# A one-layer hybrid encoder on one core: dense weight remainders formed by VectorE alone, and the spatial gating bias added by VectorE from a broadcast tile

## The reference, cut to what matters

```python
xn = rmsnorm(x, norm_mix_g);  z = xn @ w_in            # q/k, v, o, gates, u, gv, mq, branch gates
qk = silu(causal_conv(qk_raw, conv_buf, w, b))          # mLSTM branch: matrix memory, 4 heads
...
u = gelu(u_raw);  gv = layernorm(gelu(gv_raw), gmlp_norm_g, gmlp_norm_b)
w_s = where(tri, gmlp_w_s[:, :cl, :cl], 0.0)            # cl = 128 for the prompt, 64 for the sample
sp = einsum('gts,bcsgd->bctgd', w_s, gvb) + gmlp_b_s[:, :cl].T[None, None, :, :, None]
br_gmlp = (u * sp) @ w_br_gmlp
...
x = x + (gates0 * br_mlstm + gates1 * br_gmlp + gates2 * br_mem) @ w_out
x = x + hier_moe(rmsnorm(x, norm_moe_g), ...)           # 32 experts of 1024 x 256, top 2 of a group of 8
```

## Time and profile before

| | |
|---|---|
| median of 3 runs | 993.53 us |
| the profiled execution | 991.24 us |
| its span (first to last instruction) | 989.5 us |
| mean granted clock of PE | 0.97 of full speed |
| PE busy | 898.8 us (91%) |
| DVE busy | 594.8 us (60%) |
| ACT busy | 473.1 us (48%) |
| POOL busy | 250.9 us (25%) |

### The profile page before, as it was taken

The page is one execution under the profiler, slowest core; times in us unless marked ns, Lnnn a source line. Parts: engine busy times, 40 slices in busy tenths (PEclk is TensorE's granted clock), DMA queues, the critical chain, the costliest instruction groups (busy, mean ns, idle before and its releaser), DMA issues.

```text
span 989.5 us, 13338 instructions
## 1 busy us (share of the span) xinstructions
PE 898.8 (91%) x5322; PEld 796.4 (80%) x5322; DVE 594.8 (60%) x794; ACT 473.1 (48%) x571; POOL 250.9 (25%) x161
## 2 busy tenths in 40 slices
PE   1889999888999989888999999869999999999993
PEld 0588998878989889888999999838877887787881
DVE  2734257884133254378354444584888889889874
ACT  4344345442433133334323333357777677767752
POOL 3145543333442444243443444100000000000000
PEclk9999999998999999989999999969999999999996
DMA  8225642333347856943423348204999999999951
GB/s 244 85 91 166 213 154 81 97 97 116 123 148 97 108 157 88 138 139 119 148 88 126 128 128 276 108 0 174 350 353 348 352 347 343 350 348 355 348 201 56
DMA packets 102502, 182.68 MB, mean 185 GB/s; under 512 B 8345, under 2 KB 74593, under 8 KB 102434
## 3 DMA queue, kind: packets, MB, share of 16 engines
q1 hardware_dynamic: 95488, 171.55, 54.2%
q0 software_dynamic: 2640, 7.66, 3.6%
q10 hardware_dynamic: 4306, 2.54, 1.3%
HBM read 175.90 MB, written 5.82 MB: 184 GB/s over the span
## 4 chain that ended last, share of the span: by engine, by line
PE 55%; DMA 10%; DVE 5%; ACT 4%; POOL 2%; issue 2%; DVEq 0%; SPq 0%; ACTq 0%
PE pj L526 25%; PE pj L776 14%; PE pj L798 8%; DMA arena<-in_w_in 8%; POOL unit_r L1586 2%; DMA arena<-in_w_exp_down 2%; ACT unit_r L882 2%; PE ms L812 1%; PE ms L700 1%; PE ms L699 1%; ACT w_r L889 1%; DMA arena<-in_w_exp_up 1%; PE ms L526 1%; PE ms L741 1%; DVE w_r L1183 1%
## 5 line engine op out<-in xcount | busy, mean ns | idle before, releaser
L1586 POOL TENSOR_TENSOR unit_r<-arena,unit_r 128x1024 fp32r<-128x1024 f32 x64 | 210.4, 3289 | 326.9 <-ACT unit_r L882 326.9
L526 PE MATMUL pj<-xn_r,unit_r 128*128 128x320 f32 x1536 | 237.3, 313 | 9.6 <-POOL unit_r L1586 9.0
L1183 DVE TENSOR_TENSOR w_r<-arena,w_r 128x2048 fp32r<-128x2048 f32 x96 | 218.9, 2289 | 44.5 <-ACT w_r L889 44.2
L526 PEld LDWEIGHTS pj<-xn_r,unit_r 128*128 128x128 f32 x1536 | 228.4, 190 | 14.1 <-issue 12.7
L1174 DVE TENSOR_TENSOR unit_r<-arena,unit_r 128x1024 fp32r<-128x1024 f32 x64 | 85.0, 1329 | 233.5 <-ACT unit_r L882 233.5
L889 ACT ACTIVATE w_r<-arena 128x2048 fp32r<-128x2048 f32 x96 | 183.5, 1917 | 46.1 <-DMA arena<-in_w_exp_up 30.7
L776 PE MATMUL pj<-w_r,xg 128*128 128x512 f32 x768 | 190.8, 398 | 0.0
L776 PEld LDWEIGHTS pj<-w_r,xg 128*128 128x128 f32 x768 | 141.9, 189 | 30.5
L882 ACT ACTIVATE unit_r<-arena 128x2048 fp32r<-128x2048 f32 x64 | 121.9, 1905 | 62.2 <-PE pj L526 28.9
L798 PE MATMUL pj<-w_r,hidT 128*128 128x512 f32 x384 | 93.1, 391 | 3.0 <-DVE w_r L1183 1.5
L798 PEld LDWEIGHTS pj<-w_r,hidT 128*128 128x128 f32 x384 | 71.6, 188 | 20.1 <-DVE w_r L1183 3.6
(11 more groups left out here) (303 smaller groups left out, 844.9 us busy)
## 6 DMA issues: line engine op xcount, KB each, us to landing
arena<-in_w_in SPq DMA_DIRECT2D x40, 1024.0 KB, 5.3
arena<-in_w_exp_gate SPq DMA_DIRECT2D x64, 512.0 KB, 4.5
arena<-in_w_exp_up SPq DMA_DIRECT2D x64, 512.0 KB, 6.0
arena<-in_w_exp_down SPq DMA_DIRECT2D x64, 512.0 KB, 5.2
arena<-in_w_mem_k SPq DMA_DIRECT2D x4, 1024.0 KB, 11.3
arena<-in_w_mem_v SPq DMA_DIRECT2D x4, 1024.0 KB, 6.3
arena<-in_w_br_mem SPq DMA_DIRECT2D x4, 1024.0 KB, 7.7
arena<-in_w_br_mlstm SPq DMA_DIRECT2D x4, 1024.0 KB, 5.0
```

The lines of the kernel that those rows point to most:

```text
L526: last = mm(bank_of(s)[0:out_rows, 0:out_cols], l, r, start=k == 0, stop=k == len(pairs) - 1)
L1183: v.tensor_tensor(w_r[u % NS][:, 1, :], raw_w[u % NS], w_r[u % NS][:, 0, :], ALU.subtract).then_inc(m_lo, 1)
L1586: g.tensor_tensor(unit_r[n % RING][:, 1, UW // 2:], ringw[:, n % RING, UW // 2:], unit_r[n % RING][:, 0, UW // 2:], ALU.subtract).then_inc ...
```

## The change

Two edits. First, DVE forms the whole rest of a dense unit (2048 columns), and POOL none; the two counters `u_lo` become one. Second, the bias of the spatial gating leaves PE: `bsb`, loaded on ACT's queue, holds gmlp_b_s in all 128 rows (256 KB in place of 2 KB). In an sp step DVE adds it to the bank's 256 prompt columns and 64 sample columns into `spb` (in the memory of `h_tm`, free once the heads are transposed), which frees the bank, waits for that, and multiplies `uT` by `spb`. ACT then waits for the product's own semaphore `s_spm`. The third tile's matmul runs over 128 rows, for which DVE zeroes rows 64 to 127 of `gv_tm`'s third tile ahead of the statistics.

```diff
@@ -354,7 +354,8 @@
         wr = sb("wr", [128, KC, G + E])
         wrb = sb("wrb", [G + E, 1])
         wif = sb("wif", [128, KC, 2 * H])
-        bs = sb("bs", [1, H * 128])
+        bsb = sb("bsb", [128, H, 128])
+        spb = at(XS, T)
         ws2 = sb("ws2", [128, 2 * H, 128])
         ws, wsT = ws2[:, 0:H, :], ws2[:, H:2 * H, :]
         nf_g = ws2[:, :, :].rearrange("p a b -> p (a b)")
@@ -411,12 +412,13 @@
         s_c1s = sem("C1_sample_ready")
         s_hn = sem("h_scaled")
         s_mix, s_wsT = sem("gate_used"), sem("wsT_masked")
+        s_bs, s_spm = sem("spatial_bias_loaded"), sem("u_gated")
         s_gng, s_gnd, s_gvout = sem("gn_loaded"), sem("gv_normed"), sem("gv_out")
 
         s_nfg, s_gm = sem("nf_g_loaded"), sem("moe_g_loaded")
         s_lgx, s_lge, s_route, s_pone = sem("router_arg"), sem("router_exp"), sem("routed"), sem("expert_weights_split")
         s_hnh, s_hnl = sem("hn_high"), sem("hn_rest")
-        u_hi, u_lo = sem("unit_high_part"), {"D": sem("unit_rest_first_half"), "P": sem("unit_rest_second_half")}
+        u_hi, u_lo = sem("dense_unit_high"), sem("dense_unit_rest")
         s_xnh, s_xnl, s_mnh, s_mnl = sem("xn_high"), sem("xn_rest"), sem("mn_high"), sem("mn_rest")
         s_avh, s_hTh, s_hTl = sem("attention_high"), sem("heads_high"), sem("heads_rest")
         s_uh, s_ul, s_mixh, s_mixl = sem("u_high"), sem("u_rest"), sem("mixture_high"), sem("mixture_rest")
@@ -469,8 +471,7 @@
             sp.dma_start(srows[48:56, :], I["state_mlstm_n"][0, 0].rearrange("h (c p) -> (h c) p", p=128)).then_inc(s_par2, 16)
             for n, (name, col) in enumerate(UNITS):
                 if n >= RING:
-                    for e in "DP":
-                        sp.wait_ge(u_lo[e], n - RING + 1)
+                    sp.wait_ge(u_lo, n - RING + 1)
                 src = I[name][0, :, col:col + 256].rearrange("(k p) n -> p k n", p=128)
                 sp.dma_start(ringw[:, n % RING, :].rearrange("p (k n) -> p k n", n=256), src).then_inc(unit_full[n % RING], 16)
 
@@ -692,12 +691,10 @@
                 elif kind == "sp":
                     c, = a
                     g = c // 2
-                    pe.wait_ge(s_par3, 16 * 5)
                     pe.wait_ge(s_gnd, 3)
                     pe.wait_ge(s_wsT, 1)
                     for i, (t0, n) in enumerate(TILES):
-                        mm(b[:, t0:t0 + n], gv_tm[0:n, i, c * 128:c * 128 + 128], wsT[0:n, g, 0:n], start=True, stop=False)
-                        last = mm(b[:, t0:t0 + n], ones128[0:1, :], bs[0:1, g * 128:g * 128 + n], start=False, stop=True)
+                        last = mm(b[:, t0:t0 + n], gv_tm[:, i, c * 128:c * 128 + 128], wsT[:, g, 0:n], start=True, stop=True)
                 elif kind == "hnT":
                     i, half = a
                     n = TILES[i][1]
@@ -866,7 +863,7 @@
             act.wait_ge(s_mem, 32)
             for i in range(2):
                 af(mnT[:, 4 * i:4 * i + 4, :].rearrange("p a b -> p (a b)"), mem_tm[:, i, :], ACT.Square, accum_out=ssx[:, 3 + i:4 + i]).then_inc(s_ss, 1)
-            act.dma_start(bs[:, :], I["gmlp_b_s"][0].rearrange("(a g) t -> a (g t)", a=1)).then_inc(s_par3, 16)
+            act.dma_start(bsb[:, :, :], I["gmlp_b_s"][0].partition_broadcast(128)).then_inc(s_bs, 16)
             act.dma_start(ws[:, :, :], I["gmlp_w_s"][0].rearrange("g t s -> t g s")).then_inc(s_ws, 16)
             act.dma_start(wr[:, :, 0:G], I["w_router_group"][0].rearrange("(k p) n -> p k n", p=128)).then_inc(s_par3, 16)
             act.dma_start(wr[:, :, G:G + E], I["w_router_expert"][0].rearrange("(k p) n -> p k n", p=128)).then_inc(s_par3, 16)
@@ -1005,7 +1002,7 @@
                     af(br_r[:, 0, :, t0:t0 + n], oT[:, :, t0:t0 + n], ACT.Copy).then_inc(s_hTh, 1)
                 elif kind == "sp":
                     c, = a
-                    act.wait_ge(*done("sp", c))
+                    act.wait_ge(s_spm, c + 1)
                     if c == 0:
                         act.wait_ge(s_c1out, 32 * H)
                         act.wait_ge(s_s1out, 32 * H)
@@ -1171,7 +1168,7 @@
             def unit_second_part(n):
 
                 dve.wait_ge(u_hi, n + 1)
-                v.tensor_tensor(unit_r[n % RING][:, 1, 0:UW // 2], ringw[:, n % RING, 0:UW // 2], unit_r[n % RING][:, 0, 0:UW // 2], ALU.subtract).then_inc(u_lo["D"], 1)
+                v.tensor_tensor(unit_r[n % RING][:, 1, :], ringw[:, n % RING, :], unit_r[n % RING][:, 0, :], ALU.subtract).then_inc(u_lo, 1)
 
             def rest(dst, x, high, count, value, signal):
                 dve.wait_ge(count, value)
@@ -1349,6 +1346,7 @@
                 elif kind == "gv_norm":
                     heads_rest(2)
                     dve.wait_ge(*done("gv", 3, 2))
+                    v.memset(gv_tm[64:128, 2, :], 0.0)
                     for i, (t0, n) in enumerate(TILES):
                         for q in range(2):
                             ins = v.bn_stats(bst[0:n, i, 6 * q:6 * q + 6], gv_tm[0:n, i, 512 * q:512 * q + 512])
@@ -1368,7 +1366,17 @@
                 elif kind == "sp":
                     c, = a
                     dve.wait_ge(*done("u", c))
-                    v.tensor_tensor(uT[:, c, :], uT[:, c, :], b[:, 0:T], ALU.mult).then_inc(free, 1)
+                    if c == 0:
+                        dve.wait_ge(s_bs, 16)
+                        dve.wait_ge(*done("hT", 2, 1))
+                    else:
+                        dve.wait_ge(s_spm, c)
+                    g = c // 2
+                    v.tensor_tensor(spb[:, 0:TP].rearrange("p (i t) -> p i t", t=128), b[:, 0:TP].rearrange("p (i t) -> p i t", t=128),
+                                    bsb[:, g:g + 1, :].to_broadcast([128, 2, 128]), ALU.add)
+                    v.tensor_tensor(spb[:, TP:T], b[:, TP:T], bsb[:, g, 0:TS], ALU.add).then_inc(free, 1)
+                    dve.wait_ge(*done("sp", c))
+                    v.tensor_tensor(uT[:, c, :], uT[:, c, :], spb[:, :], ALU.mult).then_inc(s_spm, 1)
                     for j in range(max(c - 1, 0), c if c < 7 else 8):
                         rest(u_r[:, 1, j, :], uT[:, j, :], u_r[:, 0, j, :], s_uh, j + 1, s_ul)
                 elif kind == "br":
@@ -1581,18 +1589,12 @@
             def load_cache_v(h):
                 pool.dma_start(cmv[:, h % 2, :, :], I["cache_mem_v"][0, 0, :, h, :].rearrange("(j p) d -> p j d", p=128)).then_inc(s_cachev[h % 2], 16)
 
-            def unit_second_part(n):
-                pool.wait_ge(u_hi, n + 1)
-                g.tensor_tensor(unit_r[n % RING][:, 1, UW // 2:], ringw[:, n % RING, UW // 2:], unit_r[n % RING][:, 0, UW // 2:], ALU.subtract).then_inc(u_lo["P"], 1)
-
             def load_state(h):
                 pool.dma_start(C0[:, h % 2, :, 0:HD], I["state_mlstm_C"][0, 0, h].rearrange("(k p) e -> p k e", p=128)).then_inc(s_c0[h % 2], 16)
 
             for h in range(2):
                 load_cache_k(h)
                 load_cache_v(h)
-            unit_second_part(0)
-            unit_second_part(1)
             for s in STEPS:
                 kind, a = s["kind"], s["args"]
                 if kind == "bc":
@@ -1645,8 +1647,6 @@
                 elif kind == "u" and a[0] == 7:
                     pool.wait_ge(s_gnd, 3)
                     pool.dma_start(O["gmlp_v_sample"][0, 0], gv_tm[0:64, 2, :]).then_inc(s_gvout, 16)
-                if s["ring"] == "pj" and s["last"] and s["unit"] + RING < len(UNITS):
-                    unit_second_part(s["unit"] + RING)
 
             pool.wait_ge(s_nfg, 16)
             pool.wait_ge(s_mout, 32)
```

More of the change, by code:

```diff
@@ L488, in load_unit @@
                     elif u == 4:
-                        for e in "DP":
-                            sp.wait_ge(u_lo[e], len(UNITS))
+                        sp.wait_ge(u_lo, len(UNITS))
                 else:
@@ L544, in _ @@
                     n = s["unit"]
-                    for e in "DP":
-                        pe.wait_ge(u_lo[e], n + 1)
+                    pe.wait_ge(u_lo, n + 1)
                     w = unit_r[n % RING][:, :, :].rearrange("p a (k n) -> p a k n", n=256)
@@ L709, in _ @@
                     pe.wait_ge(*done("hnT", 2, 1))
-                    pe.wait_ge(s_par3, 16 * 5)
+                    pe.wait_ge(s_par3, 16 * 4)
                     last = project(s, G + E, T, [(wr[:, k, :], hnT[:, k, :]) for k in range(KC)])
@@ L1414, in _ @@
                         hn_rest(0, i)
-                    dve.wait_ge(s_par3, 16 * 5)
+                    dve.wait_ge(s_par3, 16 * 4)
                     dve.wait_ge(ready["ms"], s["at"] + 1)
```

## The result

The changed kernel took 952.31 us in the median of 4 runs (948.43 to 953.76), the kernel before 991.43 beside it (4 runs): a ratio of 0.9596, 95% interval 0.9547 to 0.9645. The forecast was 968 with a range of 956 to 979: the sign was right, the gain too small. The profiled executions stand at 989.5 and 952.0 us of span, 37.5 apart, where my terms gave 24.8.

A forecast was written before the change was run, and what follows sets the result against it. PE, busy 91%, was taken as the bound, with its waits in the dense part to win. Terms 3.8, 1.2, 4.0, 6.4, 1.1, 9.5 and minus 1.2 summed to 24.8 us, giving 968, range 956 to 979.

The forecast's parts named there:

- Prologue: Start of the kernel: scalings without POOL halves beside them bring the parameter copy 3.9 us sooner; 3.8 taken.
- bias load: Prologue, ACT's queue: the 256 KB bias tile delays ACT's first square root; minus 1.2 us, bounds 0 and 2.5.
- Convolutions: 16 blocks on 8 units: shorter DVE steps and copies, longer wholes; 4.0 us gained with scalings, bounds 0 and 9.6.
- The wait at 59: PE's wait of 2.93 us ending at 59.08: its last link comes sooner, gaining 1.2 us.
- Ring chain: PE's waits before 350.24 and 424.07: last link and earlier outputs give 3.2 us each, 6.4 together, bounds 2.3 to 10.8.
- the two ways of sharing: Ring chain: DMA engines go round queues packet by packet (6.4 us gained) or queues share by time (4.6).
- The place at 451: PE's wait of 2.73 us before 451.48: last link sooner, memset added; 1.1 us gained, bounds 0.3 and 2.
- Bias matmuls: The sp steps, 476 to 545: L700's matmuls leave PE, 1.19 us in each of 8 steps, 9.5 gained.
- more goes than I count: Rival: all POOL waits, the convolution waits, prologue, bias and load go, 39 us, giving 954; chance 0.17.
- The rival of bias and prologue alone: DVE comes to its wholes as late as POOL's halves ended; only 12.1 us go, giving 981; chance 0.13.
- the slower one: Rival: DVE's long steps aren't POOL's doing; 15 us of losses against the bias's 9.5, giving 999; chance 0.03.
- the wait near 345: Sign of being wrong, at the first ring place: the forecast is wrong if this PE wait keeps its length.

The follow-up runs named there:

- e1: Kernel before with only the unit rests changed (DVE subtracts all 2048 columns, POOL none), bias matmuls kept: 968.59 us, ratio 0.9734 to before.
- e9: Kernel after with the n states gathered, transposed and written as rows of 128 bytes instead of 4-byte writes: 947.58 us, ratio 0.9646 to before.
- e3: Kernel after with the third tile contracting over 64 rows again and without the memset: 957.35 us.
- e7: Kernel after with POOL subtracting 2 x 512 columns of a private tile beside every unit, nobody waiting for it: 964.15 us, ratio 0.9741 to before.
- e12: Kernel after with bias tile and router loads moved from ACT's queue in the prologue to POOL's queue later, repeat of e8: 943.44 us, ratio 0.9610 to before.
- e11: Kernel after run again unchanged, in a set where the kernel before took 982.30: 949.89 us, ratio 0.9677 to before.
- e5: Kernel after leaving out the eight 4-byte-run writes of the n states: 948.14 us, ratio 0.9576 to before.
- e6: Kernel before leaving out the same n state writes, POOL halves kept: 976.74 us, ratio 0.9858 to before.
- e14: Kernel before leaving out the n state writes, repeat of e6 in another set: 975.60 us, ratio 0.9937 to before.
- e2: Kernel before with only the bias edit (bias tile and adds on DVE, third tile over 128 rows), POOL halves kept: 984.74 us, ratio 0.9890 to before.
- e4: Kernel after with the bias added on PE again by matmuls over 128 rows, DVE multiplying straight from the bank: 961.55 us.
- e8: Kernel after with bias tile and router loads moved from ACT's queue in the prologue to POOL's queue behind the memory outputs: 944.62 us, ratio 0.9549 to before.

## Why the forecast came out too small

The sum, 24.8, is 12.7 short of the profiled pair: 4.1 in the bias matmuls, 3.0 in the two waits that were taken at their length (59 and 451), 1.6 in the ring chain, 0.9 in prologue and convolutions, and 3.1 in places that the sum doesn't hold. Term by term:

- *Prologue, 3.8 less 1.2 for the bias load: 3.3 measured.* e1 without the large load gained 3.9 there. That puts the bias load at 0.6, and ACT's queue took 8.7 us for its six issues where it took 8.0 before. But kernels with the prologue of the kernel after start their gate projections anywhere from 30.9 (e9) to 32.5 us (e3), so its cost is known no better than its bounds of 0 and 2.5, and no run shows the share that the forecast took as hidden by the queue's depth.
- *Convolutions, 4.0: 4.2.* Right, and by the mechanism named: 48 x (722 - 556) = 8.0 and 16 x (509 - 159) = 5.6 won, 8 x 1.07 = 8.6 lost on the wholes, 5.0 net on DVE. e7 shows that it is POOL's work in SBUF and not the wait for it.
- *The wait at 59, 1.2: 2.8.* The wait itself gave 1.3. The step that failed is that a wait's worth was taken as its length: the matmuls behind it gave 1.5 more, nearly all in the next 29, at a granted clock of 1.00 instead of 0.65. It is no accident of one execution: the 72 matmuls behind this wait took 10.35 to 11.55 us in the four profiles with POOL's halves (wait 2.9), and 8.86 in eleven of the twelve without (wait 1.6), 10.36 in e12 (wait 1.8).
- *Ring chain, 6.4: 8.0 in the profiled pair,* as -0.2 at 350 and 8.2 at 424 (6.3 of wait, 1.9 of clock), not 3.2 and 3.2. That the two add up to something near the forecast is luck. What became of the assumption "the outputs leave 1 to 2.8 sooner, and the load ends sooner by as much" can be read from POOL's issues, here before (the one of 324.71 is in the earlier trace rows), after, and in e11, the kernel after again:

```profile
326.15 0.73 POOL L1641 DMA_DIRECT2D out_mlstm_C_sample<-arena  x1
395.95 0.73 POOL L1641 DMA_DIRECT2D out_mlstm_C_prompt<-arena  x1
```

```profile
313.50 0.71 POOL L1643 DMA_DIRECT2D out_mlstm_C_prompt<-arena  x1 [27.34 <-ACT arena L978]
316.78 0.71 POOL L1643 DMA_DIRECT2D out_mlstm_C_sample<-arena  x1 [1.85 <-DVE arena L1323]
381.62 0.72 POOL L1643 DMA_DIRECT2D out_mlstm_C_prompt<-arena  x1 [24.02 <-ACT arena L978]
```

```profile
313.01 0.71 POOL L1643 DMA_DIRECT2D out_mlstm_C_sample<-arena  x1 [0.38 <-DVE arena L1323]
```

PE is 10.24 and 10.07 us ahead at the two places, and against that the prompt outputs at 350 left 1.0 sooner, but the sample outputs 0.9 later. They waited for DVE behind one of its own wholes, which began 1.6 later after a load of 19.79 us where the kernel before had 16.95. The next load took 20.76 us instead of 19.84, and the wait stayed. At 424 the prompt outputs left 4.3 sooner and the whole wait went. In e11 the sample outputs at the first place left 3.0 sooner than in the kernel after, against PE, and there was no wait. So the outputs' start counts, as forecast, but it is not settled by the edit: it moves with the execution. Neither place moved by 3.2 or by 2.3, so these runs can't choose between the two ways of sharing that the forecast weighed. e5 and e6 show the base of both: loads slowed by the n writes. The size of this term changes too; where the kernel before took 982 instead of 991 to 994, the change was worth 32.4 instead of 39.1. Without n writes (e14 and e6 against e5, partly across sets) it is worth 27.5 to 28.6, and this part, ring places left out, I had forecast at 18.4.
- *The place at 451, 1.1: 2.5.* 1.0 by the wait, and 1.5 by the clock behind it (0.74 before, 1.00 after). Above the bound of 2, for the same reason as at 59, but here the loss is not in every execution: behind the same wait of 2.73 the 144 matmuls took 22.88 us in the kernel before and in e6, and 21.37 in e14, as fast as behind 1.72.
- *Bias matmuls, 9.5: 13.6.* The largest miss. "The third tile now contracts over 128 rows instead of 64, with the same columns: I put 0, bounds 0 and 0.5" failed, and so did the price of L700 as its own rows' alone. The rows that stay got 0.50 a step shorter. The chain showed it: L699 held 11.6% of 69 us, 1.0 us a step, for six passes that cost 0.1 each where no row count changes. That price stood in the same trace: six transposes of 128 rows (L654) took PE from 268.30 to 268.88.
- *Not in the sum:* 1.0 in branch 1, of which 0.8 in three gate steps of 7.31 us that became 7.04; the wait list doesn't hold it. e1 has this gain and e2 not, so it is the unit edit's. And 1.5 in w_out, where the granted clock was 0.95 before and 1.00 after behind the same wait of 2.2; e3, e4 and e7 show it too, e1, e2, e5 and e8 don't. It is chance and not the change: e11, the kernel after again, took 35.7 us for these matmuls as the kernel before did, and e14, with POOL's halves, the 34.2 of the kernel after.

The rival "more goes than I count" came nearest to the time (954), and not by its way: it took all POOL waits and all of the convolution wait, of which 6.4 and 4.7 stayed. The rival of bias and prologue alone (981) fell with the 4.2 of the convolutions and the 8.0 of the ring places, the slower one with the convolution step's 556 ns. One sign of being wrong came true: the wait near 345 kept its length (4.49, then 4.66).

## What to carry to other kernels

Price a wait that goes as its length plus what PE loses behind it, and read that from the granted clock of the matmuls that follow: here 1.3 to 1.9 us behind each of the four long waits of the kernel before, but over all profiles anything from 0 to 2.7, so give it a range. Where short matmuls with different contraction rows alternate, count the changes of the row count; padding with zeros or moving the odd one to another engine can be worth more than the matmul itself (here 0.16 a change against 0.11 a pass). A wait for the last link of a chain says little on its cause: here leaving out 4-byte writes on another queue removed what the trace put down to GpSimd.

## What was not expected of the hardware

- A change of the number of contraction rows between float32 matmuls cost PE 0.16 to 0.17 us, by two kernels; a pass of 128 rows and 128 or 64 columns without one 0.11.
- 1 KB written in 4-byte pieces held 1 MB loads on another queue to 16 to 21 us, where they take 5.2 without.
- Five small parameter loads issued in the prologue kept ScalarE's next instruction back by 6 us, most of it in the issue of two whose rows are short (2.83 and 4.08 us); on GpSimd's queue later they cost nothing that shows.
